# Two norms folded or split, two gates applied part by part, and the first blocks of a three-layer kernel merged

## The chip, the cores and the metric

The kernel runs on one core of one Trainium2 chip. The metric is device microseconds of one execution; the time given for a kernel is the median of its runs. One execution is also recorded by the hardware profiler, and all rows below come from that one.

## The reference

Three layers follow each other on 256 tokens of width 1024, in fp32. What the change touches, cut to its core:

```python
def rms_norm(x, g):
    y = x * rsqrt(mean(x * x) + EPS)
    return y * g

# layer one (first_block)
h = rms_norm(x, norm_mix_g);  proj = h @ w_in        # queries, keys, values, index, gates
lam = exp(sum(lp[0] * lp[1])) - exp(sum(lp[2] * lp[3])) + lam_init
o_a = diff_attention(rope(q), rope(k), v, lam)       # rope tables: cos and sin of the positions
idx_s = sum over 8 heads of  w[h] * relu(qi[h] @ ki) # one row of scores for each token
_, sel = top_k(where(causal, idx_s, -inf), 64)       # attention over 64 chosen keys
x = x + mix @ w_out;  x = x + memory_attention(...)
x = x + peer_ffn(...)                                # 128 + 128 tables of experts
x = rms_norm(x, final_norm_g)                        # the final norm of layer one

# layer two: a hybrid mixer (l = 0), then latent attention (l = 1); after each an FFN and this:
x = x + sb_rwkv_mixer(rms_norm(x, attn_norm_2[0]), ...)
e = rms_norm(p[l] @ ple_proj[l], ple_norm_2[l])      # an embedding of each token
x = x + sigmoid(rms_norm(x, ple_gate_norm_2[l]) @ ple_gate[l]) * e
return rms_norm(x, final_norm_2)
```

## The kernel before

Activations are kept feature by feature: `x` is 8 chunks of 128 features by 256 tokens. All weights come as one stream of 512 KB groups through a ring of four slots, sent by SyncE (SP). A group is two **halves** of 128x512. For each half ScalarE (ACT) writes the high part (L349), VectorE (DVE) the low part (L355), and TensorE (PE) multiplies three times for each 128x128 block (L381 to L383): high by high, low by high, high by low. A half is four blocks, so 12 matmuls. Four halves can be split and unused at once (`SLOTS`), and a product's block splits up to three halves beyond its own end (`AHEAD`).

`products` runs one block of products. Everything that ACT and DVE do in it is a list of **duties**, each with a due time counted in halves, a priority and a kind; the list is sorted and each engine executes its own kinds in that order. So an engine that waits in one duty holds up all later ones, the splitting of weights among them:

```python
duties.sort(key=lambda d: d[:2])
```

A normed input is not normed first: the product takes `x * gain`, and the inverse root comes onto the results when they are copied out of PSUM (L811). Its squares are made in one ACT instruction (L680), PE sums them with a matrix of ones behind the first unit of four output tiles (L644), DVE makes mean and reciprocal (duty `root`, L751 and L754), ACT the square root (L685). The root duty stands one half behind the unit's end, ahead of all later splitting.

`load` (L895) sends positions, parameters, constants, x, the memory and the first four weight groups, and ends when the first three have landed. Then come a block for the rope tables (L940 to L969), one for lambda (`lambda_of`, with a DMA of its own at L1260) and the first products, which wait for all of x. All sections are separate blocks: every engine waits for all at each end.

In the first products, the two attentions of layer one and the choice of keys run as **steps** beside the gates: every engine takes a fixed number of steps per half. `together` runs the choice beside the differential attention and the norm of its heads. `choose_steps` spends steps 0 to 16 on one head each (a matmul L1361, a relu L1371, a weighted sum L1386), and steps 18 to 25 on eight rounds of choice, each with the eight largest (L1398) and their replacement (L1401) for both blocks of tokens.

Behind the experts stands `between`, a block of its own: `norm` (L863) takes squares chunk by chunk (L869), sums (L878), reciprocal (L886), root (L872) and scaling (L890) one after the other, and then the hybrid mixer's products begin with a norm of their own. `ple` runs the projection and the gate's product in one block, and then a block with the sigmoid over all eight chunks (L1932), the norm of the embedding (L1938) and two instructions of 128x2048 (L1942, L1943). `finish` calls `norm` and stores x in one DMA (L2586).

## Time and profile before

| | |
|---|---|
| median of 3 runs | 2313.42 us (2304.46 to 2321.68) |
| the profiled execution | 2314.81 us, of which the span is 2313.0 us |
| mean granted TensorE clock | 0.928 |
| PE busy | 1997.3 us (86%) |
| DVE busy | 1529.7 us (66%) |
| ACT busy | 1222.2 us (53%) |
| moved from HBM | 293.26 MB, 127 GB/s over the span |

The span is the time from the first to the last recorded instruction; 1.8 us of the profiled execution lie around it. PE's busy time counts modelled ends, so overlapping matmuls make it look fuller than the array is.

### The profile page before, as it was taken

What the parts mean: (1) busy time and instruction counts of PE and PEld (TensorE: products, weight loads), DVE (VectorE), ACT (ScalarE), POOL (GpSimd) and SP (SyncE); (2) the same over time, 40 slices, a digit from 0 to 9 for tenths busy, and PEclk for the clock granted to TensorE, in tenths of its full rate; (3) what the DMA queues carried; (4) which work ended last, traced back from release to release, by engine and by line L of the source; (5) the groups of instructions that cost most, each with busy time, mean ns of one, the idle gap of its engine ahead of it and who ended that gap; (6) DMA issues with size and microseconds to landing.
All of it is one profiled execution on the core that took longest, in us unless ns stands there. A gap on an engine that the chain in (4) does not pass through costs nothing. (4 is left out here: it accounts for less than half of the span.)

```text
span 2313.0 us, 44158 instructions
## 1 busy us (share of the span) xinstructions
PE 1997.3 (86%) x15796; PEld 1917.7 (83%) x15796; DVE 1529.7 (66%) x3122; ACT 1222.2 (53%) x2396; POOL 15.3 (1%) x21
## 2 busy tenths in 40 slices
PE   6998888999999766999999873896998968799895
PEld 5887778999999756999998863796998957799895
DVE  4657555999644688666665657765687567568755
ACT  4454554777755698555555453102555543555553
POOL 0000000000000000000000000000000001000000
PEclk9999998999999899999999996886999989799998
DMA  4422333445555301555554430001455523045441
GB/s 169 146 100 92 121 99 119 157 171 187 175 190 183 98 0 36 191 193 193 194 191 163 140 107 19 1 1 46 160 193 164 173 73 128 10 159 192 164 165 55
DMA packets 95216, 295.97 MB, mean 128 GB/s; under 512 B 9203, under 2 KB 25718, under 8 KB 94582
## 3 DMA queue, kind: packets, MB, share of 16 engines
q1 hardware_dynamic: 95094, 294.35, 37.9%
q8 instruction: 76, 1.25, 0.2%
q14 instruction: 46, 0.38, 0.1%
HBM read 293.26 MB, written 1.05 MB: 127 GB/s over the span
## 5 line engine op out<-in xcount | busy, mean ns | idle before, releaser
L381 PE MATMUL bank<-a_high,w_high 128*128 128x256 f32 x3256 | 937.9, 288 | 132.2 <-DVE a_low L741 61.9
L355 DVE TENSOR_TENSOR w_low<-ring,w_high 128x512 fp32r<-128x512 f32 x1102 | 747.3, 689 | 429.3 <-ACT w_high L349 424.5
L349 ACT ACTIVATE w_high<-ring 128x512 fp32r<-128x512 f32 x1102 | 680.0, 628 | 463.6 <-PE bank L383 459.6
L382 PE MATMUL bank<-a_low,w_high 128*128 128x256 f32 x3256 | 922.4, 283 | 0.0
L383 PE MATMUL bank<-a_high,w_low 128*128 128x256 f32 x3256 | 921.8, 283 | 0.0
L381 PEld LDWEIGHTS bank<-a_high,w_high 128*128 128x128 f32 x3256 | 632.9, 194 | 150.2 <-issue 107.1
L382 PEld LDWEIGHTS bank<-a_low,w_high 128*128 128x128 f32 x3256 | 629.4, 193 | 0.4
L383 PEld LDWEIGHTS bank<-a_high,w_low 128*128 128x128 f32 x3256 | 629.7, 193 | 0.0
L381 PE MATMUL bank<-s_high,w_high 128*128 128x256 f32 x1024 | 282.7, 276 | 2.0 <-DVE s_low L1872 2.0
L383 PE MATMUL bank<-s_high,w_low 128*128 128x256 f32 x1024 | 282.6, 276 | 0.0
L382 PE MATMUL bank<-s_low,w_high 128*128 128x256 f32 x1024 | 282.6, 276 | 0.0
L381 PEld LDWEIGHTS bank<-s_high,w_high 128*128 128x128 f32 x1024 | 192.2, 188 | 2.2 <-DVE s_low L1872 2.2
L382 PEld LDWEIGHTS bank<-s_low,w_high 128*128 128x128 f32 x1024 | 192.2, 188 | 0.0
L383 PEld LDWEIGHTS bank<-s_high,w_low 128*128 128x128 f32 x1024 | 192.2, 188 | 0.0
L1790 PE MATMUL bank<-hot 128*128 128x128 f32 x512 | 80.3, 307 | 45.4 <-ACT hot L1736 37.4
L1790 PEld LDWEIGHTS bank<-hot 128*128 128x128 f32 x512 | 68.6, 209 | 57.4 <-issue 29.6
L1538 ACT ACTIVATE arena<-bank 128x256 f32 x128 | 49.2, 384 | 84.9 <-PE bank L383 84.0
L1727 ACT ACTIVATE hn<-consts,hn 128x128 f32<-128x128 f32 x256 | 81.7, 390 | 11.9 <-PEq L1673 4.3
L1761 DVE TENSOR_SCALAR hot<-consts,hn 128x128 f32<-128x128 f32 x256 | 71.0, 342 | 1.4 <-PEq L1673 0.4
L1041 PE MATMUL bank<-arena 64*128 64x128 f32 (+4 forms) x144 | 46.2, 417 | 17.5 <-PEq L1961 11.3
L2504 ACT ACTIVATE arena<-bank 64x256 f32<-64x256 f32 x8 | 3.0, 378 | 100.4 <-PE bank L2472 100.3
L1872 DVE TENSOR_TENSOR s_low<-arena,s_high 128x256 fp32r<-128x256 f32 x128 | 53.4, 418 | 0.8 <-ACT s_high L1852 0.8
(309 smaller groups left out, 2033.4 us busy)
## 6 DMA issues: line engine op xcount, KB each, us to landing
ring<-in_stream SPq DMA_DIRECT2D x279, 512.0 KB, 3.6
ring<-in_peer_u SPq DMA_DIRECT2D x128, 512.0 KB, 3.5
ring<-in_peer_v SPq DMA_DIRECT2D x128, 512.0 KB, 3.4
ring<-in_stream SPq DMA_DIRECT2D x32, 256.0 KB, 3.2
consts<-in_consts SPq DMA_DIRECT2D x1, 1024.0 KB
x<-in_x SPq DMA_DIRECT2D x1, 1024.0 KB, 7.1
arena<-in_mem SPq DMA_DIRECT2D x1, 1024.0 KB, 9.1
out<-x SPq DMA_DIRECT2D x1, 1024.0 KB, 4.0
```

The source lines that it names most:

```text
L349: self.nc.scalar.activation(self.w_high[:, h % SLOTS, :], self.raw(h), ACT.Copy)\
L355: self.nc.vector.tensor_tensor(self.w_low[:, h % SLOTS, :], self.raw(h), self.w_high[:, h % SLOTS, :].bitcast(F32), ALU.subtract)\
L381: self.nc.tensor.matmul(to, lh, rh, start=start, stop=False, **more)
L382: self.nc.tensor.matmul(to, lh, rl, start=False, stop=False, **more)
L383: return self.nc.tensor.matmul(to, ll, rh, start=False, stop=stop, **more)
L1041: nc.tensor.matmul(scores(f), q, k, start=True, stop=True).then_inc(scored.up(), 1)
L1538: nc.scalar.activation(to, self.bank[k % 4][:, 0:T], ACT.Gelu)\
L1727: ins = nc.scalar.activation(distance[:, b % 2, i, :], iota, ACT.Abs, scale=-1.0, bias=number)
L1761: ins = nc.vector.tensor_scalar(hot[:, 1, b, i, :], iota, one(1), one(2), ALU.is_equal, ALU.mult)
L1790: ins = nc.tensor.matmul(self.bank[b][:, i * P:(i + 1) * P], hot[:, 0, b, i, :], hot[:, 1, b, i, :], start=True, stop=True)
L1872: nc.vector.tensor_tensor(s_low[:, k % SIDES, :], self.arena[:, bass.ds(it * (RING * T) + k * T, T)], s_high[:, k % SIDES, :].bitcast(F32) ...
L2504: nc.scalar.activation(y[64 * p:64 * p + 64, :, L * n:L * n + L], quarter(2 + p, 64 * p), ACT.Copy).then_inc(y1.up(), 1)
```

## The change

Five edits. (1) `load` takes lambda's row, sends the constants and x in parts and the memory last; lambda is computed in the rope tables' block; inputs wait for their own part of x. (2) The key choice takes two heads in a step and spends 16 steps on its eight rounds, one for the largest and one for their replacement. (3) The embedding's norm, the sigmoid and the gating become duties of the products' block, the last two for two tiles at a time. (4) `between` is gone: a source of kind `Twice` takes x times the product of both gains, and the root is made from two sums, since `mean((x*g1*r)^2) = r*r*mean((x*g1)^2)`; x itself is normed later by `whole` duties. (5) `finish` takes squares and the gain two chunks or one at a time on ACT, the root's scaling and the store in four parts.

```diff
@@ products @@
+        if applied(len(units) - 1):
+            duties += [(units[norms[1][2]].end + 4, 4, "embed", c) for c in range(DC)]
...
+                    key = max(end(u, h) + late, soon)
+                    duties.append((key, 3, "unit", (u, h)))
+                    if applied(u):
+                        key = max(key, units[norms[1][2]].end + 4)
+                        duties += [(key + 1, 4, "sigmoid", (u, h)), (key + 2, 4, "apply", (u, h))]
...
+                            for c in range(norm.chunks if isinstance(norm, Twice) else 0):
+                                nc.tensor.matmul(self.bank[6][:, 0:T], self.const("ones"),
+                                                 norm.squares[:, c, :], start=c == 0,
+                                                 stop=c == norm.chunks - 1)
...
+                        if isinstance(norm, Twice):
+                            for c in range(norm.chunks):
+                                nc.scalar.activation(norm.squares[:, c, :], norm.source[:, c, :],
+                                                     ACT.Square, scale=self.param(norm.first, c))
...
+                    elif kind == "sigmoid":
+                        u, h = what
+                        act.wait_ge(copied[1].sem, copied[1].at(copies(u, h, 1)))
+                        nc.scalar.activation(half(u, h)[1], half(u, h)[1], ACT.Sigmoid)\
+                            .then_inc(spread.up(), 1)
                     elif kind == "root":
                         act.wait_ge(mean.sem, mean.at(what + 1))
+                        if isinstance(norms[what][0], Twice):
+                            nc.scalar.activation(inverse[1], inverse[1], ACT.Sqrt)
                         nc.scalar.activation(inverse[what], inverse[what], ACT.Sqrt)\
...
+                        if isinstance(norms[what][0], Twice):
+                            link(nc.vector.tensor_scalar(inverse[1], summed[what], 1.0 / D, EPS,
+                                                         ALU.mult, ALU.add))
+                            link(nc.vector.reciprocal(inverse[1], inverse[1]))
+                            link(nc.vector.scalar_tensor_tensor(
+                                out=inverse[0], in0=self.bank[6][:, 0:T], scalar=1.0 / D,
+                                in1=inverse[1], op0=ALU.mult, op1=ALU.mult))
+                            link(nc.vector.tensor_scalar(inverse[0], inverse[0], EPS, None, ALU.add))
+                            link(nc.vector.reciprocal(inverse[0], inverse[0]))
+                            nc.vector.tensor_tensor(inverse[0], inverse[0], inverse[1], ALU.mult)\
+                                .then_inc(mean.up(), 1)
+                            continue
                         link(nc.vector.tensor_scalar(inverse[what], summed[what],
...
+                    elif kind == "embed":
+                        place = units[-1].place
+                        dve.wait_ge(root.sem, root.at(2))
+                        ins = nc.vector.scalar_tensor_tensor(
+                            out=place.by[:, what, :], in0=place.by[:, what, :],
+                            scalar=self.param(place.gain, what), in1=inverse[1], op0=ALU.mult,
                             op1=ALU.mult)
+                        if what == DC - 1:
+                            link(ins)
+                    elif kind == "apply":
+                        u, h = what
+                        n = units[u].tile + 2 * h
+                        place, to = units[u].place, half(u, h)[1]
+                        dve.wait_ge(spread.sem, spread.at(sum(applied(v) and (v, i) <= (u, h)
+                                                              for v, i in parts)))
+                        link(nc.vector.tensor_tensor(to, to, place.by[:, n:n + 2, :], ALU.mult))
+                        nc.vector.tensor_tensor(place.to[:, n:n + 2, :], place.to[:, n:n + 2, :], to,
+                                                ALU.add)
                     elif kind == "gated":
                         u, phase = what
...
@@ load @@
+                sp.dma_start(self.params[:, :], self.dram["params"]).then_inc(loaded.up(16), 16)
+                sp.dma_start(self.at(70 * T, 1)[0:1, 0, :], self.dram["da_lambda"])\
+                    .then_inc(loaded.up(16), 16)
+                sp.dma_start(self.consts[:, 0:soon, :], self.dram["consts"][:, 0:soon, :])\
+                    .then_inc(loaded.up(16), 16)
+                for c in range(4):
+                    sp.dma_start(self.x[:, 2 * c:2 * c + 2, :], self.dram["x"][:, 2 * c:2 * c + 2, :])\
+                        .then_inc(self.x_landed[c], 16)
+                for g in range(2):
+                    self.send(sp, g, g, self.group(g))
+                sp.dma_start(self.consts[:, soon:, :], self.dram["consts"][:, soon:, :])\
+                    .then_inc(self.consts_landed, 16)
+                for g in range(2, RING):
+                    self.send(sp, g, g, self.group(g))
+                self.sent = RING
...
@@ rope_tables @@
+                    for i in range(2):
+                        r = lambdas[:, 128 * i:128 * i + 128]
+                        ins = nc.vector.tensor_tensor(prod[:, 64 * i:64 * i + 64], r[:, 0:64],
+                                                      r[:, 64:128], ALU.mult)
+                    link(ins)
+                    nc.vector.tensor_reduce(dot[:, 0:2],
+                                            prod[:, 0:128].rearrange("p (i d) -> p i d", i=2), AX,
+                                            ALU.add).then_inc(dots.up(), 1)
...
+                if lam is not None:
+                    act.wait_ge(weights.sem, weights.at(1))
+                    nc.scalar.activation(lam[:, 1:3], self.bank[1][:, 0:2], ACT.Exp)\
+                        .then_inc(exps.up(), 1)
...
@@ choose_steps @@
+        pairs = [(0, 2), (4, 6), (1, 3), (5, 7)] * 2
+        keys = lambda f: (f // 4 + 1) * P
+        part = lambda f: idx[:, 2 + 2 * (f % 2):4 + 2 * (f % 2), 0:keys(f)]
+        scores = lambda f: self.bank[bank][:, 0:2 * keys(f)].rearrange("p (h s) -> p h s", h=2)
...
-                if 18 <= i < 18 + N_SEL // 8:
+                if i in range(10, 10 + 2 * (N_SEL // 8), 2):
                     for b in range(TT):
                         ins = nc.vector.max(out=best[:, 8 * b:8 * b + 8], in_=total(b))
                     link(ins)
+                if i in range(11, 11 + 2 * (N_SEL // 8), 2):
...
@@ ple, hybrid @@
-                      after=(self.fetched, self.fetched.total))
-        inverse = self.small[:, T:2 * T]
-        opened = self.counter("gate_open")
-        with nc.Block(no_gpsimd_drain=True) as block:
-            @block.scalar
-            def _(act):
-                nc.scalar.activation(gate, gate, ACT.Sigmoid).then_inc(opened.up(), 1)
-
-            @block.vector
-            def _(dve):
-                link = self.chain(dve, "dve")
-                for c in range(DC):
-                    link(nc.vector.scalar_tensor_tensor(
-                        out=e[:, c, :], in0=e[:, c, :], scalar=self.param(f"ple_norm_2.{l}", c),
-                        in1=inverse, op0=ALU.mult, op1=ALU.mult))
-                dve.wait_ge(opened.sem, opened.at(1))
-                link(nc.vector.tensor_tensor(e, e, gate, ALU.mult))
-                nc.vector.tensor_tensor(x[:, :, :], x[:, :, :], e, ALU.add)
+                        Applied(lambda n, c: gate[:, n:n + c, :], e, f"ple_norm_2.{l}", x))],
+                      also=Normed(e, f"ple_norm_2.{l}"), after=(self.fetched, self.fetched.total))
...
-        h = Normed(x, "attn_norm_2.0")
+        h = Twice(x, "final_norm_g", self.pair_gain, place(8))
+        free[0] -= 8 * T
...
@@ finish @@
+                nc.scalar.activation(self.small[:, T:T + 1], self.const("ones")[:, 0:1], ACT.Sqrt)
+                for c in range(0, DC, 2):
+                    nc.scalar.activation(hn[:, c:c + 2, :], x[:, c:c + 2, :], ACT.Square)\
+                        .then_inc(squares.up(), 1)
+                act.wait_ge(squares.sem, squares.at(DC // 2))
+                for c in range(DC):
+                    if c == 6:
+                        act.wait_ge(mean.sem, mean.at(1))
+                        nc.scalar.activation(inverse, inverse, ACT.Sqrt).then_inc(root.up(), 1)
+                    nc.scalar.activation(x[:, c, :], x[:, c, :], ACT.Copy,
+                                         scale=self.param("final_norm_2", c)).then_inc(gained.up(), 1)
+
...
+                for c in range(0, DC, 2):
+                    sp.wait_ge(ready.sem, ready.at(c // 2 + 1))
+                    sp.dma_start(self.out[:, c:c + 2, :], x[:, c:c + 2, :]).then_inc(stored.up(16), 16)
```

Three places show how the instructions move.

SP in `load`, before (`ring` are the weight slots, `arena` of the first row the positions, of the last the memory):

```order
L901 DMA arena<-in_positions 1x256
L904 DMA params<-in_params 128x355
L904 DMA consts<-in_consts 128x2048
L905 DMA x<-in_x 128x2048
L906 DMA arena<-in_mem 128x2048
L313 DMA ring<-in_stream 128x1024 x4
```

and with the change:

```order
L991 DMA arena<-in_positions 1x256
L993 DMA params<-in_params 128x355
L994 DMA arena<-in_da_lambda 1x256
L996 DMA consts<-in_consts 128x768
L999 DMA x<-in_x 128x512 x4
L334 DMA ring<-in_stream 128x1024 x2
L1003 DMA consts<-in_consts 128x1280
L334 DMA ring<-in_stream 128x1024 x2
L1008 DMA arena<-in_mem 128x2048
```

SP has 14 transfers to issue where it had nine, before the block can end.

DVE in the block of the hybrid mixer's first products, with the change, from the last splitting ahead of the root (L376 is the splitting that was L355, `small` holds the inverse roots, L900 is the copy out of PSUM that was L811):

```order
L376 TENSOR_TENSOR w_low<-ring,w_high 128x512 x7
L810 TENSOR_SCALAR small<-bank 128x256
L812 RECIPROCAL small<-small 128x256
L813 SCALAR_TENSOR_TENSOR small<-bank,small 128x256
L816 TENSOR_SCALAR small<-small 128x256
L817 RECIPROCAL small<-small 128x256
L818 TENSOR_TENSOR small<-small 128x256
L376 TENSOR_TENSOR w_low<-ring,w_high 128x512 x2
L900 TENSOR_TENSOR arena<-bank,small 128x512 x2
L376 TENSOR_TENSOR w_low<-ring,w_high 128x512 x2
L840 SCALAR_TENSOR_TENSOR x<-x,params,small 128x256
L376 TENSOR_TENSOR w_low<-ring,w_high 128x512
L840 SCALAR_TENSOR_TENSOR x<-x,params,small 128x256
```

Before, only one mean and one reciprocal (L751, L754) stood between the two rows of splitting. Four more DVE instructions stand there now.

DVE in the block of the second embedding, before (L811 is the copy out of PSUM):

```order
L355 TENSOR_TENSOR w_low<-ring,w_high 128x512 x2
L811 TENSOR_TENSOR arena<-bank,small 128x512 x2
L355 TENSOR_TENSOR w_low<-ring,w_high 128x512 x4
L811 TENSOR_TENSOR arena<-bank,small 128x512 x2
L540 UNCONDITIONAL_BRANCH
L1934 UNCONDITIONAL_BRANCH
L1938 SCALAR_TENSOR_TENSOR arena<-arena,params,small 128x256 x8
L1942 TENSOR_TENSOR arena<-arena 128x2048
L1943 TENSOR_TENSOR x<-x,arena 128x2048
```

and with the change (L847 norms the embedding, L859 and L860 apply the gate):

```order
L376 TENSOR_TENSOR w_low<-ring,w_high 128x512 x2
L900 TENSOR_TENSOR arena<-bank,small 128x512 x2
L376 TENSOR_TENSOR w_low<-ring,w_high 128x512
L847 SCALAR_TENSOR_TENSOR arena<-arena,params,small 128x256 x8
L376 TENSOR_TENSOR w_low<-ring,w_high 128x512 x2
L859 TENSOR_TENSOR arena<-arena 128x512
L860 TENSOR_TENSOR x<-x,arena 128x512
L859 TENSOR_TENSOR arena<-arena 128x512
L860 TENSOR_TENSOR x<-x,arena 128x512
L376 TENSOR_TENSOR w_low<-ring,w_high 128x512
L900 TENSOR_TENSOR arena<-bank,small 128x512
L859 TENSOR_TENSOR arena<-arena 128x512
```

The norm's eight instructions now stand ahead of the splitting of the last three halves, and four of the gate's ahead of the last one's. In the first embedding's block the order is the same, with three more halves split behind, for the next block.

## Rows read from the trace of the kernel before

**Rows 1.** The page, part 1: engine, busy us, share of the span, instructions.

```profile
PE 1997.3 (86%) x15796; PEld 1917.7 (83%) x15796; DVE 1529.7 (66%) x3122; ACT 1222.2 (53%) x2396; POOL 15.3 (1%) x21
```

**Rows 2.** The timeline, SP: start us, us, engine, line, operation.

```profile
0.75 0.35 SPq L901 DMA_DIRECT2D arena<-in_positions  x1
...
2.99 2.17 SPq L313 DMA_DIRECT2D ring<-in_stream  x4
```

**Rows 3.** The timeline of the first blocks, in brackets the idle time before.

```profile
7.13 0.28 DVE L940 CAST arena<-arena 1x256 f32<-1x256 int32 x1 [7.13 <-PEq L898]
...
14.11 0.63 ACT L969 ACTIVATE arena<-arena 128x512 f32<-128x512 f32 x1 [5.74 <-DVE arena L957]
...
18.79 1.70 ACT L659 ACTIVATE a_high<-x,params 128x256 fp32r<-128x256 f32 x4 [0.72 <-PEq L1257]
```

**Rows 4.** Busy time and granted clock by stretch, beside the gates.

```profile
120.00:170.00 50.00, 49.66 (x324) 39.53 (x324) 27.25 (x78) 26.10 (x80) 0.00 (x0) 1.00 0.25 85
178.30:203.40 25.10, 16.55 (x99) 15.36 (x99) 24.39 (x72) 9.53 (x17) 0.00 (x0) 0.80 0.19 64
```

**Rows 5.** DVE's instructions by line in 178.3 to 203.4: busy us, mean ns.

```profile
L1401 DVE MATCH_REPLACE8 arena<-arena 128x128 f32<-128x128 f32 (+1 forms) x14 | 4.7, 343 | 0.0
L1398 DVE MAX8 arena<-arena 128x8 f32<-128x128 f32 (+1 forms) x14 | 4.3, 346 | 0.1
...
L1401 DVE MATCH_VALUE_LOAD arena<-arena 128x8 f32 x14 | 1.2, 87 | 0.2
```

**Rows 6.** The timeline, PE, after a short pause beside the gates.

```profile
180.62 0.36 PE L381 MATMUL bank<-a_high,w_high 128*128 128x256 f32 x1 [1.87 <-DVE w_low L355]
...
181.44 0.42 PE L383 MATMUL bank<-a_high,w_low 128*128 128x256 f32 x1
```

**Rows 7.** The timeline, norm of layer one to the hybrid's first products.

```profile
1263.67 0.72 ACT L869 ACTIVATE arena<-x 128x256 f32<-128x256 f32 x2 [3.49 <-PEq L1813]
...
1277.20 3.30 ACT L659 ACTIVATE a_high<-x,params 128x256 fp32r<-128x256 f32 x8 [3.63 <-PEq L863]
...
1278.37 0.55 PE L381 MATMUL bank<-a_high,w_high 128*128 128x256 f32 x1 [7.50 <-DVE a_low L736]
...
1282.20 1.13 ACT L349 ACTIVATE w_high<-ring 128x512 fp32r<-128x512 f32 x2
...
1283.42 0.36 PE L383 MATMUL bank<-a_high,w_low 128*128 128x256 f32 x1
```

**Rows 8.** The timeline, sums and root in the hybrid's first products.

```profile
1291.80 3.62 PE L644 MATMUL bank<-hn,consts 128*128 128x256 f32 x16
...
1295.91 1.75 DVE L754 RECIPROCAL small<-small 128x256 f32<-128x256 f32 x1
...
1299.41 0.38 PE L381 MATMUL bank<-a_high,w_high 128*128 128x256 f32 x1 [1.26 <-DVE w_low L355]
```

**Rows 9.** The timeline, DVE, the two embedding blocks.

```profile
1859.76 1.89 DVE L355 TENSOR_TENSOR w_low<-ring,w_high 128x512 fp32r<-128x512 f32 x3
...
1874.21 2.29 DVE L1943 TENSOR_TENSOR x<-x,arena 128x2048 f32<-128x2048 f32 x1
...
2284.52 0.69 DVE L811 TENSOR_TENSOR arena<-bank,small 128x512 f32<-128x512 f32 x1 [3.49 <-PE bank L383]
...
2292.09 2.29 DVE L1943 TENSOR_TENSOR x<-x,arena 128x2048 f32<-128x2048 f32 x1
```

**Rows 10.** The timeline of the last norm.

```profile
2295.19 6.73 PE L878 MATMUL bank<-arena,consts 128*128 128x256 f32 x16 [10.78 <-ACT arena L869]
...
2301.19 1.28 ACT L872 ACT_TABLE_LOAD   x1
...
2304.66 3.25 DVE L890 SCALAR_TENSOR_TENSOR x<-x,params,small 128x256 f32<-128x256 f32 x8 [0.48 <-ACT small L872]
```

**Rows 11.** The transfers: tensor, queue, count, KB each, us from issue to landing.

```profile
out<-x SPq DMA_DIRECT2D x1, 1024.0 KB, 4.0
...
arena<-in_ple SPq DMA_DIRECT2D x2, 256.0 KB, 2.5
```

More of the change, by code:

```diff
@@ L136, with __init__ @@
 class Normed:
-    def __init__(self, source, gain, chunks=DC, size=D):
+    def __init__(self, source, gain, chunks=DC, size=D, ready=()):
         self.source, self.gain, self.chunks, self.size = source, gain, chunks, size
+        self.ready = ready
+class Twice(Normed):
+    def __init__(self, source, first, gains, squares):
+        super().__init__(source, None)
+        self.first, self.gains, self.squares = first, gains, squares
 class Times:
@@ L147, in __init__, with __call__ @@
         self.place, self.factor, self.first = place, factor, first
+class Applied:
+    def __init__(self, place, by, gain, to):
+        self.place, self.by, self.gain, self.to = place, by, gain, to
+    def __call__(self, n, c):
+        return self.place(n, c)
 class Steps:
@@ L426, in products, with gain, applied @@
                   for i, (s, _, _) in enumerate(norms)]
+        def gain(source, c):
+            if isinstance(source, Twice):
+                return source.gains[:, c:c + 1]
+            return self.param(source.gain, c)
+        def applied(u):
+            return isinstance(units[u].place, Applied)
         def normed(u):
@@ L767, in _ @@
                         norm = norms[0][0]
+                        twice = isinstance(norm, Twice)
                         dve.wait_ge(root.sem, root.at(1))
@@ L929, in _ @@
             def _(sp):
-                if here:
+                if lam is not None:
                     return
@@ L1420, in memory @@
         work = self.at(24 * T, 8)
[L1421 to L1422 removed]
+        self.products([("mem_q", "fm", Normed(x, "norm_mem_g"), lambda n, c: q[:, n:n + c, :])])
         flat = self.at(32 * T, 2, 512)
@@ L1896, in expert_sum @@
         self.taken += N_KEYS * BLK
-    def between(self):
-        x = self.x
-        self.norm(lambda c: x[:, c, :], lambda c: self.param("final_norm_g", c),
-                  lambda c: x[:, c, :])
     def ffn(self, l):
@@ L2578, in finish @@
         nc = self.nc
-        x = self.x
-        self.norm(lambda c: x[:, c, :], lambda c: self.param("final_norm_2", c),
-                  lambda c: x[:, c, :])
-        stored = self.counter("stored")
-        with nc.Block(no_gpsimd_drain=True) as block:
+        x, hn = self.x, self.hn
+        squares, sums, mean, root, gained, ready, stored = (
+            self.counter(s) for s in ("squares_ready", "square_sums_ready", "mean_ready", "root_ready",
+                                     "gained", "output_ready", "stored"))
@@ new lines, in finish, with _ @@
+        inverse, total = self.small[:, 0:T], self.bank[7][:, 0:T]
+        with nc.Block(no_gpsimd_drain=True) as block:
+            @block.scalar
+            def _(act):
+                nc.scalar.activation(self.small[:, T:T + 1], self.const("ones")[:, 0:1], ACT.Sqrt)
[9 more added lines that the diff above has]
+                                         scale=self.param("final_norm_2", c)).then_inc(gained.up(), 1)
+            @block.tensor
+            def _(pe):
+                for c in range(DC):
+                    pe.wait_ge(squares.sem, squares.at(c // 2 + 1))
+                    ins = nc.tensor.matmul(total, self.const("ones"), hn[:, c, :], start=c == 0,
+                                           stop=c == DC - 1)
+                ins.then_inc(sums.up(), 1)
+            @block.vector
+            def _(dve):
+                link = self.chain(dve, "dve")
+                dve.wait_ge(sums.sem, sums.at(1))
+                link(nc.vector.tensor_scalar(inverse, total, 1.0 / D, EPS, ALU.mult, ALU.add))
+                nc.vector.reciprocal(inverse, inverse).then_inc(mean.up(), 1)
+                dve.wait_ge(root.sem, root.at(1))
+                for c in range(0, DC, 2):
+                    dve.wait_ge(gained.sem, gained.at(c + 2))
+                    nc.vector.tensor_tensor(x[:, c:c + 2, :], x[:, c:c + 2, :], inverse.unsqueeze(1)
+                                            .broadcast_to([P, 2, T]), ALU.mult).then_inc(ready.up(), 1)
```

151 lines of the change are left out of this document (67 added, 84 removed).

## The prediction

> **What bounds it now.** I read the granted clock and the page first, then the timelines of the places that the diff touches. PE is busy 86% of the span [rows 1], the other engines far less, so I ask at each place whether PE waits and for whom. Beside the gates PE is full from 120 to 170 while DVE works 27 of 50 us; from 178.3 to 203.4 it turns over, DVE is busy 24.4 of 25.1 us, PE has 99 matmuls where it did 324 in twice the time, and its mean granted clock is 0.80 [rows 4]. Between the experts and the hybrid's products, behind both embedding products and at the end, PE has next to nothing to do: these stretches are chains of DVE and ACT [rows 7, 9, 10].
>
> Two more things to see. At full rate, 2.4 GHz, a block's three matmuls take 0.34 us, a half 1.36 us; at 1.2 GHz each takes 0.21 us. After the long pause before the hybrid's products PE was at the low level for 5.05 us, until 1283.42 [rows 7]: 24 matmuls, that would have taken 2.7 us. So each such start costs 2.35 us. A pause of 1.87 us was enough for the fall [rows 6], one of 1.26 us was not [rows 8].
>
> **Start.** DVE begins when the constants have landed, at 7.13 [rows 3], long after SP's last issue. The changed block needs less data but ends only when SP has issued 14 transfers. Five issues took from 0.75 to 2.99, 0.45 us each, and four of weights 0.54 each [rows 2]: 10 x 0.45 + 4 x 0.54 = 6.7, so SP is through at 7.4 and the tables start at 7.8, 0.65 later than now, given 0.35 for a change of blocks (2294.38 to 2295.19 holds one and a square of 0.42 [rows 9, 10]). The chain from L940 to the sine's end stays 7.6 us [rows 3]; lambda's few small instructions stand in DVE's wait for PE, the exponential and its table in ACT's wait for the angles. Inputs then start at 15.7 instead of 18.79 [rows 3]: **3.0 saved**. Were SP's issues free, it would be 5; were a table load left on the chain, 1.7.
>
> **Choice of keys.** In 178.3 to 203.4 stand 7 rounds; a round's search costs 4.3/7 = 0.61, its replacement (4.7 + 1.2)/7 = 0.84 [rows 5]. Spread over 16 steps, 3 searches and 4 replacements remain there: 4 x 0.61 + 3 x 0.84 = **5.0 saved**, since DVE is the bound and PE, with eight halves (11 us) to do, stays behind it. What moves ahead falls into 120 to 170, where DVE has 23 us free [rows 4]; so do the pairs of heads. Bounds: 0 if the earlier steps take it back, 6 with the first round too.
>
> **Norm of layer one.** Removed: 1263.67 to 1277.20, 13.5 us [rows 7]. Added, in order:
> - ACT squares eight more chunks, 0.41 each as for L659 [rows 7], 3.3 us, ahead of its first splitting, which was 5.0 after the block's start and is now at 8.3; with both splittings (0.63 each) the fourth half is there at 9.5. PE starts at 1.17 and its three halves last 5.05 at the low clock and 12 matmuls at the high: 7.6. It waits 1.9.
> - A second set of sums, 16 passes more: 3.5 us [rows 8], on PE's path.
> - The root: DVE adds 0.5 + 0.3 + 1.8 + 0.45 to one mean and one reciprocal (1.75 [rows 8]), and ACT a second square root of 0.4: 3.5 us. PE has only two halves (2.7 us) in hand there and already waits 1.26 [rows 8]; now 4.8.
> - After 4.8 us the clock falls: 2.35.
>
> Together 11.3, **net 2.2 saved**. The eight `whole` duties cost nothing: 0.41 + 0.61 for splitting per half of 1.36, with 0.6 for a copy in each fourth. Without the first wait and the clock's fall it is 6.5 saved; with a fall at both pauses 0.
>
> **Embeddings.** The block after the products, from the last copy's end to 2294.38 [rows 9], is replaced by one sigmoid and one application (0.65 + 1.3). But the twelve instructions ahead of the last splittings use up PE's lead. Second embedding, which runs as the first does, 417.9 later: the first of the three splittings of [rows 9] ends at 2278.2; then comes the norm of eight chunks at 0.41 (the pitch of L890 [rows 10]) to 2281.5, then the next half at 2282.2. PE ended its last half at 2284.4 and so began the third-last, which this is, at 2280.3: a wait of 2. Then two applications, 2.6, and the last half at 2286.0, another wait of 1. With the clock at 1.2 GHz between them PE ends at about 2288.5 instead of 2284.4. Copy, sigmoid and application follow: 2291.3, against 2294.4: **3.0 saved**. The first embedding splits three halves more before its last copy, as it did already, and there DVE's own chain decides: from 1859.76, seven splittings 4.3, norm 3.3, four applications 5.2, two copies 1.3, 1.4 of waits for sigmoids: 1875.3 against 1876.5, **1.2 saved**. Bounds for both: 2 and 14.
>
> **End.** The first square waits for a table load of 1.28 [rows 10] and a dummy root, 1.7 together; the sums keep PE's 6.73, all at 1.2 GHz. Scaling takes 4 x 0.61 instead of 3.25, the block change (0.7 before the store) goes, and of the store only a quarter lies behind the last part: 2.5 to land for 256 KB against 4.0 for 1024 [rows 11]; for a store behind three others I take 3.1. So -1.7 + 0.8 + 0.7 + 0.9, and 0.2 less waiting: **0.9 saved**; bounds -1 and 2.
>
> The Trainium skill (ScalarE: Activation LUTs, "Table sets: the hidden batching unit") puts a switch of sets at about 2.7 us and advises against mixing functions; by that the end would gain nothing and the total be 1.4 us less. The trace's 1.28 decides. The skill (DMA: Bandwidth & Descriptors, "Anatomy of one DMA") gives about 2.0 us plus bytes/436e9 for a transfer issued by GpSimd, an estimate of 2.6 here, 0.5 us better than my term; no row shows a small store.
>
> **Sum.** 3.0 + 5.0 + 2.2 + 3.0 + 1.2 + 0.9 = 15.3. The profiled execution has 2314.8 and would be 2299.5; it stands 1.4 above the median of 2313.4, so the median is **2298.1**. Of some 37 us by which the stretches alone shrink (3.0 + 5.0 + 13.5 + 14.4 + 0.9) less than half is left; the rest is given back as pauses of PE.
>
> **Rivals.**
> - The lead of three halves is enough and the additions hide (15%): hybrid 13.5 - 3.5 = 10, embeddings 2 x 7.2, the rest 8.9: 33 saved, 2280. For it, PE seldom waits for splitting elsewhere; against it, DVE's order shows 3.3 us of norm in one piece, and 1.26 of pause already with 2.25 of root.
> - The choice gives nothing (13%): the stretch is as long because the earlier steps, with two heads each, become the bound. 2303. For it, DVE is at its limit in single steps; against it, 23 us free.
> - Slower (4%): behind the pause of 4.8 us PE's clock stays at 1.2 GHz instead of rising after 24 matmuls. 552 matmuls follow in this block at 0.1 us more each: all gains are gone from about 150 of them, and with all the time is 2351. In the trace the low level never lasted once PE was kept full.
>
> **Chances and range.** My forecast gets 68%. Alone, with its terms' bounds taken together, it holds 2289 to 2306. Stretched towards the first rival and by a little above for the second: **2284 to 2308**. About 1% (23 us) is what a measurement here tells from no change: faster by more than that, below 2290.3, is the first rival and a tail of mine, 22%; slower by more 3%; within 75%.
>
> **What would show it.** Right: first input near 15.7; between the experts and the hybrid's first matmul 4.2 us instead of 17.8; a second L644-like group of 16 passes and a pause near 4.8 us behind it, with the granted clock low for some 5 us; two pauses of PE, 2 and 1 us, in each embedding's last unit; sums of the last norm starting 2.1 us after the block's start. Wrong: if PE's pauses in these places are below 1 us, the time is nearer 2280; if DVE is as full and as long beside the gates, nearer 2303; if the constants' landing and not SP's issues ends `load`, 1 to 2 us better.

## The result: 1.3% slower, by a thing that no step of the change computes

The changed kernel takes 2,337.66 us, the kernel before 2,305.64 beside it; the ratio is 1.0126, with an interval of 1.0090 to 1.0161. The prediction had 2,298.1 and a range up to 2,308. One of the changed kernel's six executions took 3,794.84 us at a lower mean clock (0.889); the ratio leaves it out, and the median of the other five is 2,337.41. The profiled execution of the changed kernel took 2,340.27 us, with a span of 2,338.4.

First the steps of the change, where they were predicted. The timeline of the changed kernel's start (start us, us, engine, line, operation; in brackets the idle time before), which answers to [rows 2, 3]:

```profile
6.10 1.25 SPq L334 DMA_DIRECT2D ring<-in_stream  x2
7.39 0.59 SPq L1008 DMA_DIRECT2D arena<-in_mem  x1
...
8.54 0.28 DVE L1046 CAST arena<-arena 1x256 f32<-1x256 int32 x1 [8.54 <-PEq L988]
...
15.53 0.63 ACT L1099 ACTIVATE arena<-arena 128x512 f32<-128x512 f32 x1 [3.70 <-DVE arena L1075]
...
16.48 1.70 ACT L704 ACTIVATE a_high<-x,params 128x256 fp32r<-128x256 f32 x4 [0.32 <-PEq L1033]
```

The inputs start at 16.48 where they started at 18.79. SP is through at 7.98, not at 7.4, because an issue of weights takes 0.63 to 0.70 and the memory's 0.59.

The norm of layer one in the changed kernel, same view, against [rows 7, 8]:

```profile
1280.21 3.31 ACT L704 ACTIVATE a_high<-x,pair_gain 128x256 fp32r<-128x256 f32 x8 [3.55 <-PEq L1906]
...
1281.38 0.55 PE L402 MATMUL bank<-a_high,w_high 128*128 128x256 f32 x1 [4.03 <-DVE a_low L794]
...
1283.42 3.29 ACT L729 ACTIVATE arena<-x,params 128x256 f32<-128x256 f32 x8
1286.61 1.90 ACT L731 ACTIVATE hn<-x 128x2048 f32<-128x2048 f32 x1
1288.41 2.18 ACT L370 ACTIVATE w_high<-ring 128x512 fp32r<-128x512 f32 x4
...
1289.80 0.39 PE L402 MATMUL bank<-a_high,w_high 128*128 128x256 f32 x1 [2.55 <-DVE w_low L376]
...
1305.63 0.43 DVE L810 TENSOR_SCALAR small<-bank 128x256 f32<-128x256 f32 x1 [8.33 <-PE bank L687]
...
1312.93 0.58 PE L402 MATMUL bank<-a_high,w_high 128*128 128x256 f32 x1 [4.52 <-DVE w_low L376]
```

All of it is there as described: 4.3 us from the last expert product to the first hybrid one, a wait for splitting behind the eight squares, and a wait for the longer root.

The end, same view, against [rows 10]:

```profile
2321.99 1.28 ACT L2657 ACT_TABLE_LOAD   x1 [1.77 <-PEq L577]
...
2324.06 6.11 PE L2673 MATMUL bank<-hn,consts 128*128 128x256 f32 x16 [6.09 <-ACT hn L2659]
...
2332.90 2.50 DVE L2686 TENSOR_TENSOR x<-x,small 128x512 f32<-128x512 f32 x4 [0.48 <-ACT small L2665]
2333.62 2.14 SPq L2693 DMA_DIRECT2D out<-x  x4
```

So no step went far wrong in its own place. The time went where the change edits nothing: into the expert sum, one uninterrupted stream of matmuls L381 to L383 (now L402 to L404). Busy time by stretch (stretch, its length, busy us and instruction count of PE, PEld, DVE, ACT and POOL, granted clock, DMA share, GB/s), over that sum, of the kernel before:

```profile
912.40:1260.30 347.90, 347.90 (x3069) 347.90 (x3070) 219.19 (x383) 200.25 (x382) 0.00 (x0) 1.00 0.56 192
```

and of the changed one:

```profile
912.00:1276.80 364.80, 364.76 (x3069) 364.76 (x3070) 219.25 (x383) 200.48 (x382) 0.00 (x0) 1.00 0.56 183
```

The same 3,069 matmuls, the granted clock at full in both, PE never waiting: 347.9 us before, 364.8 now. That is 113.4 ns from one matmul's start to the next against 118.9; by the start times of neighbours themselves, where records that are missing from a trace don't count, 113.3 against 118.3. The page has 3 x (3,256 + 1,024) = 12,840 such matmuls. Over a whole trace the mean start-to-start time, which I call the **pace** below, was 114.8 ns before and 118.3 after. 12,840 x 3.5 ns = 45 us lost; take off the 15.3 us that the steps were to save (what they do save is measured below), and the kernel is 30 us slower. Measured: 32.

What else does the change do? One line of it allocates `pair_gain`, 32 bytes a partition, behind `small`. All arenas and the split inputs `a_high`, `a_low`, `s_high`, `s_low`, allocated later, stand 32 bytes further on; the weights `w_high`, `w_low`, allocated earlier, don't. The kernel before has its weights at byte 49,280 and a_high at 168,512, a distance that leaves 192 when divided by 256; in the changed kernel it leaves 224. I call that remainder the **distance**. All split inputs share one distance in each kernel, and w_high and w_low stand a multiple of 256 apart.

### The profile page after: what moved, and what is told of

It is laid out like the page before. It is cut to its first block and busy times, and to the rows that moved or that the text cites. A ratio compares the mean times of both kernels' runs of the same rounds, so it can differ in the third digit from the quotient of the medians.

```text
span 2338.4 us, 44104 instructions
## 1 busy us (share of the span) xinstructions
PE 2039.5 (87%) x15796; PEld 1964.9 (84%) x15796; DVE 1530.8 (65%) x3133; ACT 1223.2 (52%) x2399; POOL 15.4 (1%) x21
## 5 line engine op out<-in xcount | busy, mean ns | idle before, releaser
L402 PE MATMUL bank<-a_high,w_high 128*128 128x256 f32 x3256 | 945.9, 291 | 139.6 <-DVE a_low L799 61.7
L376 DVE TENSOR_TENSOR w_low<-ring,w_high 128x512 fp32r<-128x512 f32 x1102 | 748.8, 689 | 462.2 <-ACT w_high L370 452.8
L404 PE MATMUL bank<-a_high,w_low 128*128 128x256 f32 x3256 | 930.4, 286 | 0.0
L402 PEld LDWEIGHTS bank<-a_high,w_high 128*128 128x128 f32 x3256 | 631.6, 194 | 155.9 <-issue 100.9
L404 PEld LDWEIGHTS bank<-a_high,w_low 128*128 128x128 f32 x3256 | 631.0, 194 | 0.0
L402 PE MATMUL bank<-s_high,w_high 128*128 128x256 f32 x1024 | 288.5, 282 | 2.0 <-DVE s_low L1965 2.0
L404 PE MATMUL bank<-s_high,w_low 128*128 128x256 f32 x1024 | 288.4, 282 | 0.0
L403 PE MATMUL bank<-s_low,w_high 128*128 128x256 f32 x1024 | 288.4, 282 | 0.0
L402 PEld LDWEIGHTS bank<-s_high,w_high 128*128 128x128 f32 x1024 | 193.8, 189 | 2.2 <-DVE s_low L1965 2.2
L404 PEld LDWEIGHTS bank<-s_high,w_low 128*128 128x128 f32 x1024 | 193.7, 189 | 0.0
```

The costliest lines, as they stand in the source:

```text
L376: self.nc.vector.tensor_tensor(self.w_low[:, h % SLOTS, :], self.raw(h), self.w_high[:, h % SLOTS, :].bitcast(F32), ALU.subtract)\
L402: self.nc.tensor.matmul(to, lh, rh, start=start, stop=False, **more)
L403: self.nc.tensor.matmul(to, lh, rl, start=False, stop=False, **more)
L404: return self.nc.tensor.matmul(to, ll, rh, start=False, stop=stop, **more)
```

## The experiments

### Does an unused tensor do it?

Four kernels, in which only an unused tensor is added: e1_before_32 and e3_before_64 to the kernel before, e2_after_64 and e4_after_128 to the changed one.

```diff
         self.small = sb("small", [P, 512])
+        self.pad = sb("pad", [P, 8])      # e1: 32 bytes; e3: [P, 16]
```

```diff
         self.pair_gain = sb("pair_gain", [P, DC])
+        self.pad = sb("pad", [P, 8])      # e2: 64 in all; e4: [P, 24], 128 in all
```

e1_before_32:

> The kernel before with one unused tensor of 32 bytes per partition allocated after `small`, as the changed kernel's pair_gain does; nothing else differs, and every instruction is the same. It moves all arenas and a_high, a_low, s_high, s_low by 32 bytes, so that their addresses are no longer multiples of 64. Theory (place in memory): the split-weight matmuls start 118.3 ns apart everywhere instead of 113.3 in most stretches, some 12,840 of them, so 2,325 to 2,350 us, the expert sum (L381 to L383 from about 912 to 1261) some 16 us longer. Rival (the change's own order of instructions or its extra waits set the pitch): 2,300 to 2,312 us, the expert sum 349 us as before.

e3_before_64:

> The kernel before with an unused tensor of 64 bytes per partition: the arenas move from 64 over a multiple of 128 to a multiple of 128. Theory with a grain of 64 bytes: the same time as before, 2,300 to 2,312 us. Theory with a grain of 128 bytes: the share of stretches at 113.3 ns changes, so the time goes off by 5 us or more either way. Rival (placement plays no part): 2,300 to 2,312 us, so this run alone tells only the grain, and only if the 32 byte one slows.

e2_after_64:

> The changed kernel with 32 more unused bytes, 64 in all with pair_gain, so that arenas and pairs stand at multiples of 64 again. Theory (place in memory): the pitch goes back to about 113.3 ns in most stretches and the time to 2,285 to 2,298 us, which is the prediction's 2,298 less or more a few. Rival (order or waits of the change): 2,330 to 2,342 us as the changed kernel.

e4_after_128:

> The changed kernel with pair_gain and padding of 128 bytes in all, so that every buffer stands at the same distance from a multiple of 128 as in the kernel before. Theory: 2,285 to 2,300 us, equal to the run with 64 bytes if the grain is 64, else different from it and with the pattern of stretches of the kernel before. Rival: 2,330 to 2,342 us.

Measured: e1 2,354.1 us, ratio to the kernel before 1.0194 (1.0154 to 1.0233), so 32 unused bytes cost 46 us. e3 2,368.6, e2 2,355.6, e4 2,324.4 (2,303 to 2,332). The theory that placement sets the pace holds (e1 is 4 us above its range), the rival falls; but my grain of 64 bytes was wrong, since e3 and e2, both at a multiple of 64, were the slowest, and e2 and e4 lie in none of the ranges given for them. The expert sum of e1, same view and as many matmuls:

```profile
920.30:1285.10 364.80, 364.78 (x3069) 364.78 (x3070) 219.33 (x383) 200.26 (x382) 0.00 (x0) 1.00 0.56 183
```

and of e3, where the pace is 120.0 ns:

```profile
926.20:1296.10 369.90, 369.88 (x3070) 369.88 (x3071) 219.36 (x383) 200.02 (x382) 0.00 (x0) 1.00 0.55 180
```

The instructions of e1 are those of the kernel before, and its sum is the changed kernel's to 0.1 us.

The traces hold a control too. PE's sums of squares of 256 fp32 columns (L644 in the kernel before, `hn` by `consts`) read two buffers that stand still in these kernels, and their starts lie 216 ns apart in the median in every trace of this document, while the split products' pace goes from 114 to 120. So PE as such did not become slower. (In e5 and e6 below these two buffers move against each other by 64 bytes, and it is 216 ns there too: not every kind of matmul showed the effect.)

### Is it the place or the distance?

e5 moves the weights too, e6 moves weights by 64 and the rest by 128.

```diff
+        self.pad_w = sb("pad_w", [P, 16])       # e5 and e6
         self.w_high = sb("w_high", [P, SLOTS, HALF * P], F32R)
...
         self.small = sb("small", [P, 512])
+        self.pad = sb("pad", [P, 16])           # e6 only
```

e5_before_w64:

> The kernel before with an unused tensor of 64 bytes ahead of w_high, so weights and pairs both move by 64 bytes: weights at 64 over a multiple of 128, a_high, a_low, s_high, s_low at a multiple of 128. With an unused tensor of 64 bytes behind `small` alone, where only arenas and pairs stood at a multiple of 128, it took 2,368.6 us and every start-to-start of the split-weight matmuls was 120.0 ns. Theory R (what counts is how the address of the moving operand stands to that of the weights): as the kernel before, 2,300 to 2,325 us, pitch 113.3 or 117.8 ns. Theory A (what counts is where arenas and pairs stand by themselves): 2,360 to 2,375 us, pitch 120.0.

e6_before_w64_64:

> The kernel before with unused tensors of 64 bytes ahead of w_high and behind `small`: weights move by 64 bytes, arenas and pairs by 128, so both stand at 64 over a multiple of 128. Theory R: 2,360 to 2,375 us, pitch 120.0 ns, since the distance between them is a multiple of 128. Theory A: 2,300 to 2,325 us, as before.

Measured: e5 2,307.5 us, ratio 0.9988 (0.996 to 1.0016), pace 114.3; e6 2,365.1, pace 119.9. So there are two pairs, each at one distance and at two places of the weights: the kernel before and e5, both at 192, are fast; e3 and e6, both at 0, are slow. What counts is the distance between weights and moving inputs, not where either stands. The weights were never moved alone, and in each of these kernels the arenas keep the distance of the split inputs.

### What does the distance do, and what are the steps worth beside it?

e7 and e8 are padded as e2 and e1, to 96 bytes; e9 has 256 bytes in all, the distance of the kernel before.

> The changed kernel with pair_gain and padding of 96 bytes in all: arenas and pairs at 32 over a multiple of 128, weights at a multiple. Distances of 0, 64 and 96 gave pitches of 120.0, 113.3 or 117.8, and 118.3 ns. If the distance works symmetrically, 32 is as 96: 118.3 ns and 2,334 to 2,342 us. If it is a matter of which stream runs ahead, 32 may be the free one: 113.3 ns or less throughout, 2,280 to 2,295 us.

e8_before_96:

> The kernel before with 96 unused bytes behind `small`, the same place as the changed kernel with 96. The pitch is that of its partner, and the partner is 13 to 17 us faster, as at distances 96 (2,354.1 against 2,337.7) and 0 (2,368.6 against 2,355.6), since the steps of the change are worth the same wherever the buffers stand; if the steps owe their gain to the place, the difference goes off by 5 us or more.

e9_after_256:

> The changed kernel with pair_gain and padding of 256 bytes in all: arenas and pairs stand as in the kernel before to the multiple of 256, where the one with 128 bytes stood as in the kernel before to the multiple of 128 only. Theory grain 256: its pitch mixes 113.3 and 117.8 ns in about the kernel before's shares, which with some 16 us of steps saved gives 2,288 to 2,300 us. Theory grain 128 (the two paces at distance 64 come by chance of each run): 2,303 to 2,332 us, median 2,315 to 2,326, as with 128 bytes.

Then: was 64 as good as 192, and what is in between (e10 to e12, e14; only the padding's size differs)?

e10_before_128:

> The kernel before with 128 unused bytes behind `small`: distance 64 modulo 256 from the weights to arenas and pairs, where the kernel before has 192. If 64 is a worse distance than 192: pitch 117.8 ns nearly throughout, 2,325 to 2,345 us. If the two are alike and each run draws its pace: 2,300 to 2,325 us, median about 2,309.

e11_after_192:

> The changed kernel with 192 bytes in all behind `small`: distance 128 modulo 256. If only the remainder to 128 counts, as at 0: pitch 120.0 ns, 2,352 to 2,358 us. If the remainder to 256 counts and 0 is bad since both streams hit the same place, 128 is the far side and the best: 113.3 ns or less throughout, 2,270 to 2,290 us.

e12_after_224:

> The changed kernel with 224 bytes in all behind `small`: distance 160 modulo 256. If only the remainder to 128 counts, as at 32: pitch 116.7 to 117.8 ns, 2,315 to 2,325 us. If the remainder to 256 counts: at or below 113.3 ns, 2,270 to 2,295 us.

e14_after_160:

> The changed kernel with 160 bytes in all behind `small`: distance 96 modulo 256. So far 0 gave 2,355.6 us, 32 2,319.9, 64 2,324.4, 128 2,337.3, 160 2,330.0, 192 2,295.0 and 224 2,337.7. If the pattern of 128 holds with the far half worse at 0 only, 96 is as 224: 2,330 to 2,342 us, pitch 118.3 ns. If 96 is free, below 2,300.

All of it in one table: medians in us, in brackets the pace of the profiled execution in ns, worked out from the start times of all neighbouring matmuls of these lines that are 100 to 130 ns apart.

```
distance mod 256   kernel before            changed kernel         difference
  0                2368.6 (119.9)  e3       2355.6 (119.9)  e2     13.0
                   2365.1 (119.9)  e6
 32                2337.8 (117.2)  e8       2319.9 (116.9)  e7     17.9
 64                2340.5 (117.0)  e10      2324.4 (117.7)  e4     16.1
 96                                         2356.6 (119.9)  e14
128                                         2337.3 (118.7)  e11
160                                         2330.0 (117.7)  e12
192                2308.7 (114.8)           2295.0 (114.9)  e9     13.7
                   2307.5 (114.3)  e5
224                2354.1 (118.3)  e1       2337.7 (118.3)         16.4
```

Down each column 5.1 ns of pace make about 60 us. Across, at one distance, the change saves 13.0 to 17.9 us, 15.4 in the mean, where 15.3 was predicted. These are differences of medians, of which those at 64 and 224 come from executions that did not stand beside each other; with e6 in place of e3 the one at 0 is 9.5, with e5 the one at 192 is 12.5. At the old distance the changed kernel takes 2,294.97 us, ratio 0.9955 (0.9929 to 0.9981), which is 4 to 16 us saved; 2,298.1 is near that kernel's time. Its expert sum, same view:

```profile
902.70:1250.70 348.00, 347.94 (x3069) 347.94 (x3070) 219.28 (x384) 200.31 (x382) 0.00 (x0) 1.00 0.58 191
```

My expectations for single distances were mostly wrong: e7, e11, e12 and e14 lie in none of the ranges given for them, while e9 (2,288 to 2,300) and the first of e10's (2,325 to 2,345) held, and e8 is 17.9 us above its partner where 13 to 17 was expected. There is no grain of 128: 96 is as bad as 0, 64 is not as good as 192 (e10 at 2,340.5, where "alike" would have been 2,309), 128 is no free place, and 160 is not as 192. Of the eight distances 192 alone is under 2,310, and it is where the kernel before happened to stand.

### Undoing single steps

At the changed kernel's own addresses, where the pace is 118.3 in all, so that a few us can be read. e13 is u1_norm_back with 256 bytes.

```diff
# u1_norm_back, e13
+            k.between()
             k.hybrid()
...
-        h = Twice(x, "final_norm_g", self.pair_gain, place(8))
-        free[0] -= 8 * T
+        h = Normed(x, "attn_norm_2.0")
...
-                       ("hyb_v", "tm", h, lambda h, n, c: v[:, h, n * P:(n + c) * P])], whole=x)
+                       ("hyb_v", "tm", h, lambda h, n, c: v[:, h, n * P:(n + c) * P])])
# u2_ple_back: `ple`, u3_choice_back: `choose_steps`, u4_finish_back: `finish` as in the kernel before
```

u1_norm_back:

> The changed kernel with the norm of layer one between the layers again (the step `between` and the plain norm ahead of the hybrid products), all addresses kept, so the same pitch of 118.3 ns. The prediction's term for this step was 2.2 us, so 2,339.9 us (2,338.5 to 2,342); if folding costs more at its waits than it saves, 2,334 to 2,337.5.

e13_norm_back_256:

> The changed kernel with the norm of layer one between the layers again and 256 bytes in all behind `small`, distance 192 as in the kernel before. Beside the changed kernel with 256 bytes (2,295.0 us): if folding saved nothing, as the pair at distance 224 had it (2,335.3 unfolded against 2,337.7), 2,291 to 2,295 us; if it saved the prediction's 2.2, 2,297 us.

u2_ple_back:

> The changed kernel with the embedding gate in its own block again, in both layers, all addresses kept. The prediction's terms were 1.2 and 3.0 us, so 2,341.9 us; since the clock did not fall behind the 2.04 us pauses that the prediction charged, theory says 2,341.5 to 2,345. Rival (the gating beside the products costs what its block cost): 2,336 to 2,339.5.

u3_choice_back:

> The changed kernel with the 16 single scores and the joined Max8 steps of the key choice again, all addresses kept. The prediction's term was 5.0 us, so 2,342.7 us; from the pauses beside the gates in the two traces 3 to 6 us, 2,340.5 to 2,343.5. Rival (the pauses come back in other places): 2,336 to 2,339.5.

u4_finish_back:

> The changed kernel with the last norm and the store in the old form (whole squares, one store), all addresses kept, so pitch 118.3 ns. The prediction's term was 0.9 us, so 2,338.6 us; from the traces (16.4 us from the last block's start to the end against 18.3) 1.9 us, 2,339.6. Rival (the four stores cost what the parts save): 2,336 to 2,338.

Measured, against 2,337.66: u1 2,335.3 (folding costs 2.4), e13 2,295.3 beside e9's 2,295.0 (it costs nothing), u2 2,343.9 (6.2 saved), u3 2,345.5 (7.9), u4 2,337.5 (nothing). By the ranges recorded, u1's loss, u2's gain and u4's nothing were each one of the cases named; u3's gain is 2 us above its range, e13 0.3 us above the range for a fold that saves nothing. These medians scatter by 1 to 3 us, and one source of that can be read. From 312.6 us on the changed kernel, u2, u4 and e1 need 96.9 to 97.1 us for 360 split products (the 1,501st to the 1,861st start), and u1 and u3 need 93.7 for the same instructions. Busy time, clock and the rest over this stretch, of the changed kernel and of u1:

```profile
312.60:409.60 97.00, 80.11 (x530) 76.03 (x529) 48.38 (x106) 45.43 (x89) 0.00 (x0) 0.84 0.28 87
```

```profile
311.60:405.30 93.70, 76.14 (x531) 71.89 (x530) 48.36 (x107) 45.00 (x89) 0.00 (x0) 0.89 0.27 89
```

The granted clock was 0.84 in one and 0.89 in the other. So 3.4 us by which the profiled u1 is ahead are not the fold's; in its own stretch the fold costs 0.5 (below). The first two runs together say that folding the norm is worth nothing that can be measured here, the last says so of the end.

The traces narrow u2 and u3 down. In u2 the first embedding's end, to the next products, lies 1.3 us further from the expert sum than in the changed kernel, and the stretch from the last mixer's products to the end is 299.2 us against 296.2: 1.3 and 3.0. In u3 the stretch from the first product to the first one behind the gates (226.94 - 18.93, against 221.84 - 19.48) is 5.7 us longer; 3.1 more come in the next twenty us, where the same instructions took 23.2 us in u3, and 20.1 both in the changed kernel and in e1, whose key choice is the old one too. The granted clock of these twenty us was 0.85 in u3 and 1.00 in the other two. So those 3.1 are not the choice's own.

## Why the prediction was wrong, by its own steps

**The sum.** This is the step that failed. It ran from "the profiled execution has 2314.8" to 2299.5 by adding the steps, which takes for granted that the matmuls in between keep their pace. The new tensor was costed at nothing, without naming what that nothing rests on: that PE's stream is as fast from any address. It isn't, and e1 shows it by 32 bytes alone, 46 us. No rival had it either; the slower one was a clock that stays low, and the granted clock was full in the stream that grew longer, and 0.933 in the mean where it was 0.928 before.

The match of 15.3 and the table's 15.4 is in part luck. The pieces below, read from traces, come to 2.3 + 5.7 + 0 + 1.3 + 3.0 + 0.3 = 12.6: the norm's 2.2 failed, and the differences of medians carry some us of scatter. The base was a little off too: 2,313.4 was the median of three executions, and with three more it was 2,305.6.

**Could it have been seen?** The kernel before held the hint. It ran its matmuls at two paces with the clock full in both. Its busy time by stretch, in the products with the first of the experts' two tables (`peer_u`) and in the expert sum:

```profile
640.00:740.00 100.00, 100.00 (x852) 100.00 (x851) 49.13 (x71) 55.01 (x107) 0.00 (x0) 1.00 0.56 188
```

```profile
1000.00:1100.00 100.00, 100.00 (x885) 100.00 (x884) 63.02 (x111) 57.89 (x111) 0.00 (x0) 1.00 0.57 193
```

852 matmuls of one shape in 100 us here, 885 there, and nobody waiting. I read busy PE as PE with nothing to lose. The count would have told that 4% hung on something unnamed.

**Start.** 3.0 predicted, 2.3 measured (16.48 against 18.79). SP's ten other issues cost the 0.45 each that I took (4.5 us together), but the four of weights 0.68 instead of 0.54, and from SP's end to DVE's first instruction it was 0.56 instead of 0.4; right in kind.

**Choice of keys.** 5.0 predicted, 5.7 in the stage by the traces of u3 and the changed kernel, 7.9 by medians. Right: PE's pauses of over 0.4 us beside the gates come to 11.4 us in u3 and to 7.3 in the changed kernel, and what came ahead of them is small (0.7 and 1.2).

**Norm of layer one.** 2.2 predicted, nothing measured. The pieces: 12.7 removed (17.06 to 4.31, between expert sum and first product, e1 against the changed kernel), 13.5 predicted. Given back: 2.7 at the first wait (1.9 predicted), 3.4 for the sums (3.5), 3.4 at the root (3.5). The clock is the term that was too small. I charged one fall. It fell behind both waits: in the changed kernel 51 matmuls of this block were 0.21 us apart, in e1 16; 35 x 0.095 = 3.3 us, not 2.35. Together 12.8 is given back of 12.7. The prediction had this case as "with a fall at both pauses 0". From the last expert product to the last of this block the changed kernel takes 101.3 us, e1 100.8. In e9, where the first wait was 2.05 us start to start instead of 2.83, the clock did not fall behind it.

**Embeddings.** 1.2 and 3.0 predicted, 1.3 and 3.0 by the traces. PE's predicted pauses of 2 and 1 us came, 2.03 and 1.03 start to start in the first, 2.04 and 1.03 in the second. The timeline of the second, behind the eight chunks of the norm:

```profile
2308.40 3.25 DVE L847 SCALAR_TENSOR_TENSOR arena<-arena,params,small 128x256 f32<-128x256 f32 x8
...
2311.68 1.29 DVE L376 TENSOR_TENSOR w_low<-ring,w_high 128x512 fp32r<-128x512 f32 x2
2312.43 0.39 PE L402 MATMUL bank<-a_high,w_high 128*128 128x256 f32 x1 [1.77 <-DVE w_low L376]
```

The clock did not fall here, though it had been charged: PE's last products end 3.1 us later than in u2, not 4.1. And behind PE's end stand 3.7 us where I had 2.8, because the last copy (L900, at 2318.87) waits for DVE, which executes the application ahead of it. The two nearly cancel. A table load (ACT, L737, 1.28 us at 2306.94), which I had not counted, lies on no path: DVE works from 2306.60 to 2316.84 with no pause over 0.04 us. By medians the two embeddings are worth 6.2, beyond what the traces show; the 1.9 is within the scatter of these medians, and I leave it open.

**End.** 0.9 predicted, nothing by u4 (2,337.5), 0.3 by the traces (20.69 us from the last split product to the end, against 20.95). Against u4 the sums start 2.1 us later behind the last product, for the table load and the small root ahead of the squares, and from there to the end it takes 2.3 us less. The stores landed 2.5 us after their issue in the median; I had taken 3.1 for the last.

**Rivals and chances.** Neither of the two rivals among the faster cases came: PE waited where it was said to, and the choice did pay. 97% was laid on a time that is not over 1% longer, with every case built from the steps that the diff names. A version that beats both kernels exists: the changed kernel with 256 bytes in all behind `small`, 2,295.0 us, or the same with the norm unfolded, 2,295.3 (ratio 0.9927, 0.9898 to 0.9956 by its own comparison).

## What to carry to other kernels

A buffer added ahead of others is an edit to every instruction that reads them, in this kernel a dear one: before costing a change at its own steps, compare addresses, and keep the distance between a stream's two operands, or try several with an unused tensor: here the worst and the best lie 60 us of 2,300 apart. Read a full engine by its rate, not its busy share: count one shape's instructions per 100 us in places with equal clock, and where the counts differ, a cause without a name is at work. And judge a change's steps at one common pace: against 2,305 this one looked like a loss, while at each of five distances it saved 10 to 18 us.

## What the runs showed of the hardware that was not expected

- A matmul of 256 fp32r columns, each with its own weights of 128 x 128, at a granted clock of 2.4 GHz started every 113.3 to 120.0 ns, by the distance of its two operands in bytes modulo 256: 119.9 in the mean at 0 and 96, 118.7 at 128, 118.3 at 224, 117 to 118 at 32, 64 and 160, 114 to 115 at 192.
- At the distances 32, 64, 160 and 192 one program has more than one pace, and changes it in the course of an execution, for hundreds of us at a time: 113.3 or 117.8 at 192, with 68% of the neighbouring starts at 115 ns or less in the kernel before and 85% in e13. This fits the scatter of the kernel before (2,298 to 2,332 us over all its runs), but one execution of it was profiled, so it is not shown; and a steady pace does not by itself make a steady time: at 119.9 ns e2 has 2,355.2 to 2,356.4 us, and e3 2,362.1 to 2,375.3, the slower the lower the mean granted clock of the execution (0.937 down to 0.925).
- The Trainium skill (TensorE: Matmul & The Clock Gate, "Back-to-back issue gap") gives N/2.4 + 2.5 ns as the gap of isolated matmuls at full clock, by which 256 columns would take an estimate of 109.2; in a stream of weight loads and matmuls, it says, both set the spacing. No stretch with fresh weights for each matmul of 256 columns was as fast as 109.2 here, and the section has no term for addresses. The skill (SBUF — State Buffer, "SBUF: two separate sides") has it that only the port pair shared by VectorE and GpSimd causes contention among engines. No run here tests that between engines; within PE the pace of the split products depends on where their two operands lie, and there the measurement decides.
- Why the distance acts is not shown. That weight loads and moving reads of neighbouring matmuls meet in the memory would fit, since each load starts 2 to 4 ns behind the start of the matmul before (1000 to 1100 us, in six of the kernels); but nothing here measures the memory. Nor was it tried to move arenas and split inputs apart from each other.
- Pauses of PE and the clock: it fell behind a wait of 2.55 us at 1289.80, from 1291.36 on, and not behind one of 1.77 at 2312.43, while the kernel before showed it fallen behind 1.87 [rows 6].
